# Moving the latents' modulation columns one product later in a diffusion backbone layer on one Trainium2 core

## The reference

```python
m_x = split(silu(c) @ w_ada + b_ada, 9)        # shift, scale, gate of three blocks, latents
m_c = split(silu(c_ctx) @ w_ada + b_ada, 9)    # the same for the context
x   = x   + 0.5 * m_x[2] * swiglu(modulate(rmsnorm(x, g0), m_x[0], m_x[1]), ffn1_w1, ffn1_w2)
ctx = ctx + 0.5 * m_c[2] * swiglu(modulate(rmsnorm(ctx, g0), m_c[0], m_c[1]), ffn1_w1, ffn1_w2)
px  = modulate(rmsnorm(x, g1), m_x[3], m_x[4]) @ w_in      # -> q, k, v, g, u, vg
pc  = modulate(rmsnorm(ctx, g1), m_c[3], m_c[4]) @ w_in
ret_x = retention_readout(bidir_retention(rope(q), rope(k), v, states of ctx), g)
gm_x  = gelu(u) * (w_s @ layernorm(gelu(vg)) + b_s)        # per chunk of 128 positions
x   = x + m_x[5] * (concat(ret_x, gm_x) @ w_out)
x   = x + 0.5 * m_x[8] * swiglu(modulate(rmsnorm(x, g2), m_x[6], m_x[7]), ffn2_w1, ffn2_w2)
return rmsnorm(x, final_g)
```

## Time and profile before

| | |
|---|---|
| timed runs | 2182.26, 2183.96, 2188.76 us |
| profiled execution | 2187.05 us, span 2185.2 us |
| TensorE busy | 2101.5 us (96%) |
| VectorE busy | 1539.6 us (70%) |
| ScalarE busy | 681.3 us (31%) |
| GpSimd busy | 747.6 us (34%) |
| mean granted TensorE clock | 0.980 |

### The profile page before, as it was taken

The page is one execution under the profiler, slowest core; times in us unless marked ns, Lnnn a source line. Parts: engine busy times, 40 slices in busy tenths (PEclk is TensorE's granted clock), DMA queues, the critical chain, the costliest instruction groups (busy, mean ns, idle before and its releaser), DMA issues.

```text
span 2185.2 us, 28724 instructions
## 1 busy us (share of the span) xinstructions
PE 2101.5 (96%) x10408; PEld 1754.0 (80%) x10408; DVE 1539.6 (70%) x2198; ACT 681.3 (31%) x1063; POOL 747.6 (34%) x452
## 2 busy tenths in 40 slices
PE   8999989999999999989999968998999999999997
PEld 4999978888888888878888866776888888888886
DVE  4987687777777777686353465578777777777767
ACT  4234432332233323273202111235323232232322
POOL 1000053443344433263322121365434443344431
PEclk9999999999999999989999988999999999999998
DMA  7964311111101111131010332420110111101112
GB/s 301 359 239 145 126 60 46 58 58 58 53 33 58 58 58 57 68 122 58 5 54 12 134 105 89 148 105 18 58 57 30 58 58 58 58 29 58 58 39 77
DMA packets 35161, 181.35 MB, mean 83 GB/s; under 512 B 4112, under 2 KB 5392, under 8 KB 18832
## 3 DMA queue, kind: packets, MB, share of 16 engines
q1 hardware_dynamic: 32784, 163.57, 20.4%
q10 hardware_dynamic: 2304, 16.78, 2.2%
HBM read 175.09 MB, written 5.24 MB: 83 GB/s over the span
## 4 chain that ended last, share of the span: by engine, by line
PE 86%; DVE 9%; issue 1%; ACT 1%; DMA 1%; POOL 0%; SPq 0%; DVEq 0%; ACTq 0%
PE PS L1843 14%; PE PS L1845 14%; PE PS L1844 14%; PE PS L2005 12%; PE PS L2007 12%; PE PS L2006 12%; PE PS L1948 3%; DVE AS L1313 1%; DVE X L1471 1%; PE PS L1903 1%; DVE V L1779 1%; PE PS L2202 1%; DVE ACC L1180 1%; PE PS L1881 0%; DMA AW<-w_units 0%
## 5 line engine op out<-in xcount | busy, mean ns | idle before, releaser
L1471 DVE SCALAR_TENSOR_TENSOR X<-PS,GATE,X 128x512 f32<-128x512 f32 x704 | 484.5, 746 | 186.7 <-PE PS L1845 186.7
L638 POOL TENSOR_TENSOR WVL<-WR,WVH 128x512 fp32r<-128x512 f32 x168 | 238.2, 1428 | 561.2 <-ACT WVH L849 560.4
L1843 PE MATMUL PS<-PXH,W2H 128*128 128x512 f32 x672 | 266.1, 396 | 10.2 <-DVE X L1471 10.2
L2005 PE MATMUL PS<-HH,WVH 128*128 128x512 f32 x672 | 265.3, 395 | 0.0
L1845 PE MATMUL PS<-PXH,W2L 128*128 128x512 f32 x672 | 264.9, 394 | 0.0
L2007 PE MATMUL PS<-HH,WVL 128*128 128x512 f32 x672 | 264.0, 393 | 0.0
L1844 PE MATMUL PS<-PXL,W2H 128*128 128x512 f32 x672 | 263.4, 392 | 0.0
L2006 PE MATMUL PS<-HL,WVH 128*128 128x512 f32 x672 | 262.7, 391 | 0.0
L638 POOL TENSOR_TENSOR WVL<-ST,WVH 128x512 fp32r<-128x512 f32 x125 | 186.1, 1489 | 83.2 <-ACT WVH L849 83.0
L1843 PE MATMUL PS<-HH,WH 128*128 128x512 f32 x416 | 170.4, 410 | 4.3 <-DVE WL L1621 4.3
L612 POOL TENSOR_TENSOR WL<-WR,WH 128x2048 fp32r<-128x2048 f32 x20 | 93.2, 4661 | 216.2 <-ACT WH L772 216.2
(11 more groups left out here) (258 smaller groups left out, 4410.1 us busy)
## 6 DMA issues: line engine op xcount, KB each, us to landing
WR<-w_units SPq DMA_DIRECT2D x89, 1024.0 KB, 5.4
W2R<-w_units SPq DMA_DIRECT2D x44, 512.0 KB, 3.5
AW<-w_units ACTq DMA_DIRECT2D x16, 1024.0 KB, 5.0
AW<-ada_units SPq DMA_DIRECT2D x11, 1024.0 KB, 13.7
W2RB<-w_units SPq DMA_DIRECT2D x22, 512.0 KB, 3.6
AW<-w_units SPq DMA_DIRECT2D x8, 1024.0 KB, 6.6
X<-x SPq DMA_DIRECT2D x2, 2048.0 KB, 9.9
out<-OUT SPq DMA_DIRECT2D x2, 1024.0 KB, 4.2
```

The lines of the kernel that those rows point to most:

```text
L638: pool.tensor_tensor(WVL[:, slot], src, WVH[:, slot].bitcast(F32), ALU.subtract).then_inc(s_wl, 1)
L1471: dve.scalar_tensor_tensor(xv, y_bank(n)[:, :], GATE[:, 2 * f, d, 0:1], xv, ALU.mult, ALU.add).then_inc(s_fyd, 1)
L1843: pe.matmul(dst, wh, xh, start=first, stop=False)
L2005: pe.matmul(bank[:, :], wh, xh, start=first, stop=False, skip_group_check=True)
```

## The change

Five things change, all in the handling of units 20 to 35:

1. The columns of a unit are made ahead of the entry behind the second whole product after its sums, where the short `mixed` entries are not counted (`columns_at`). Before it was ahead of the second entry.
2. The sums go into two buffers in turn (`AS2[a % 2]`), so the sums of a unit wait for the columns of the unit two before, and no longer for those of the one before.
3. The load of a unit is issued by ScalarE in two halves of 512 KB, one entry after the slot of the unit before (`load_at`; two after it for one entry), each half as soon as the sums have passed the same half of the unit before. The sums wait for each half.
4. The columns go to bank 7 in place of bank 6; to make that possible the scale of norm (2, 1) goes to bank 6 and a wait of TensorE for the last unit's modulation moves from norm_sum(2, 1) to the start of the second feed-forward block.
5. The slots are other ones. Unit 20 has its sums at the third `g` product, unit 26 at the fourth `vg` product of unit 13, there between the statistics and the normalization.

```diff
--- before.py
+++ after.py
@@ -57,8 +57,8 @@
 ADA_SUMS = (15, 14, 14, 14) + (11,) * 7 + (9, 12, 12, 12, 13)
 NRING = 6
-ADA_SLOTS = ((11, 0), (11, 2), (12, 0), (12, 2), (13, 0), (13, 2), (14, 0), (14, 3), (14, 6), (15, 0), (15, 3), (15, 6),
-             (16, 0), (17, 0), (18, 0), (19, 0))
+ADA_SLOTS = ((10, 5), (11, 0), (11, 2), (12, 0), (12, 2), (13, 0), (13, 3), (14, 3), (14, 7), (15, 1), (15, 4), (15, 7),
+             (16, 1), (17, 1), (18, 1), (19, 1))
 NM = 7
 A0, B_, A1, D_ = 0, 1, 7, 6
@@ -108,6 +108,26 @@
 ADA_AT = {ADA_CTX + n: FIRST_FILL[i] + k for n, (i, k) in enumerate(ADA_SLOTS)}
+def columns_at(a):
+
+    n, whole = ADA_AT[a], 0
+    while whole < 2:
+        n += 1
+        whole += FILLS[n][1] != "mixed"
+    return n + 1
+
+
+def load_at(a):
+
+    if a == ADA_CTX:
+        return FILL["yscale", HEADS - 1, 1] + 1
+    return ADA_AT[a - 1] + (2 if FILLS[ADA_AT[a - 1]][1:] == ("vg", 1, 0) else 1)
+
+
+ADA_COLUMNS = {columns_at(a): a for a in ADA_AT}
+ADA_LOADS = {load_at(a): a for a in ADA_AT}
+
+
 SCALED = {p: [(1, 2 * (p - 11) + k) for k in range(2)] for p in range(11, 15)}
@@ -130,7 +150,7 @@
 def sums_count(a):
-    return a - 8 + len(ADA_DVE) + 1
+    return min(a, ADA_CTX - 1) - 8 + len(ADA_DVE) + 1 + 2 * max(0, a - ADA_CTX + 1)
 def layer(nc, x, ctx, c2, ada_units, w_units, w2_units, b_ada, norm_g, final_g, decay, ws, bs, cosine, sine, consts, powers, ident, out):
@@ -221,7 +241,7 @@
         V2 = at("V2", [P, NCH, UC], F32, R + 57344)
         DG2 = at("DG2", [P, 4, P], F32, R + 67584)
         AW2 = at("AW2", [P, KT, UC], F32, R + 69632)
-        AS2 = at("AS2", [P, UC], F32, R + 68608)
+        AS2 = [at(f"AS2_{j}", [P, UC], F32, R + o) for j, o in enumerate((65536, 68608))]
         DM = at("DM", [P, HEADS, P], F32, R + 65536)
         TMP = at("TMP", [P, 2, TB], F32, R + 69632)
         S0 = at("S0", [P, 2, HEADS, P], F32, R + 73728)
@@ -365,7 +385,7 @@
         def scale_bank(place, b):
-            return {(1, 0): PS[0], (1, 2): ST_BANK, (2, 2): PS[4], (3, 2): PS[0]}.get((place, b), RB_BANK)
+            return {(1, 0): PS[0], (1, 2): ST_BANK, (2, 1): ST_BANK, (2, 2): PS[4], (3, 2): PS[0]}.get((place, b), RB_BANK)
         def last_release(bank):
             return release(max(n for n in range(len(FILLS)) if n % NRING == bank))
@@ -1079,18 +1099,19 @@
             def latent_unit(u):
-                if u == ADA_CTX:
-                    act.wait_ge(s_fill, FILL["yscale", HEADS - 1, 1] + 1)
-                else:
-                    act.wait_ge(s_adv, sums_count(u - 1))
-                act.dma_start(AW2[:, :, :], ada_source(u)).then_inc(s_first[u % 8], 16)
+                for half in range(2):
+                    k = slice(4 * half, 4 * half + 4)
+                    if u == ADA_CTX:
+                        act.wait_ge(s_fill, FILL["yscale", HEADS - 1, 1] + 1)
+                    else:
+                        act.wait_ge(s_adv, sums_count(u - 1) - 1 + half)
+                    act.dma_start(AW2[:, k, :], ada_source(u)[:, k, :]).then_inc(s_first[half], 16)
             n_gate = 0
             for n, (i, name, a, b) in enumerate(FILLS):
                 ps, free = PS[n % NRING], s_free[n % NRING]
-                for u in range(ADA_CTX, N_ADA):
-                    if n == (ADA_AT[u - 1] + 2 if u > ADA_CTX else FILL["yscale", HEADS - 1, 1] + 1):
-                        latent_unit(u)
+                if n in ADA_LOADS:
+                    latent_unit(ADA_LOADS[n])
                 if n == FIRST_FILL[i] and 5 <= i < len(MIX_UNITS) - 1:
                     mix_high(i + 1)
                 if name in ("cv", "state0", "v", "vg", "kt", "o", "g", "u"):
@@ -1252,7 +1273,7 @@
             def latent_mods(a):
                 c = 16 + 2 * (a % 4)
                 dve.wait_ge(s_col, a + 1)
-                dve.tensor_tensor(MODS[:, bass.ts(a, 2), 0], PS[6][:, c:c + 2], BA[:, bass.ts(a, 2), 0],
+                dve.tensor_tensor(MODS[:, bass.ts(a, 2), 0], RB_BANK[:, c:c + 2], BA[:, bass.ts(a, 2), 0],
                                   ALU.add).then_inc(s_mods, 1)
             def gain(place):
@@ -1300,18 +1321,23 @@
             def latent_sums(a):
-                links = 15 * sums_count(ADA_CTX - 1) + 7 * (a - ADA_CTX)
-                if a > ADA_CTX:
-                    dve.wait_ge(s_col, a)
-                dve.wait_ge(s_first[a % 8], load_count(a))
+                sums, links = sums_count(a - 1), 15 * sums_count(ADA_CTX - 1) + 6 * (a - ADA_CTX)
+                acc = AS2[a % 2]
+                if a > ADA_CTX + 1:
+                    dve.wait_ge(s_col, a - 1)
                 for k in range(KT):
+                    if k % 4 == 0:
+                        dve.wait_ge(s_first[k // 4], 16 * (a - ADA_CTX + 4))
                     w, c = AW2[:, k, :], CS[:, k, 0:1]
                     if k == 0:
-                        ins = dve.tensor_scalar(AS2[:, :], w, c, None, ALU.mult)
+                        ins = dve.tensor_scalar(acc[:, :], w, c, None, ALU.mult)
                     else:
-                        dve.wait_ge(s_asum, links + k)
-                        ins = dve.scalar_tensor_tensor(AS2[:, :], w, c, AS2[:, :], ALU.mult, ALU.add)
-                    ins.then_inc(s_adv if k == KT - 1 else s_asum, 1)
+                        if k == 4:
+                            dve.wait_ge(s_adv, sums + 1)
+                        else:
+                            dve.wait_ge(s_asum, links + k - k // 4)
+                        ins = dve.scalar_tensor_tensor(acc[:, :], w, c, acc[:, :], ALU.mult, ALU.add)
+                    ins.then_inc(s_adv if k % 4 == 3 else s_asum, 1)
             dve.wait_ge(s_const, 16 * 6)
             def block_low(b):
@@ -1699,6 +1725,12 @@
                 dve.wait_ge(sums, 3)
                 dve.tensor_tensor(s4, a12, s2, ALU.subtract).then_inc(sums, 1)
+            def unit_sums(n):
+
+                for u in ADA_AT:
+                    if ADA_AT[u] == n:
+                        latent_sums(u)
+
             n_rope = n_gate = 0
             for n, (i, name, a, b) in enumerate(FILLS):
                 ps, free = PS[n % NRING], s_free[n % NRING]
@@ -1771,6 +1803,7 @@
                     link(ins)
                     if b == 3:
                         dve.tensor_scalar(MS[:, 16:32], MV[:, :, 1], EPS, None, ALU.add).then_inc(s_lv, 1)
+                        unit_sums(n)
                         dve.wait_ge(s_lr, a + 1)
                         for c in range(NCH):
                             for g in range(2):
@@ -1808,20 +1841,20 @@
                         dve.wait_ge(s_lo[1], unit_count(DVE_UNIT))
                         dve.wait_ge(s_raw1, 16)
                         second_sums()
-                for u in range(ADA_CTX, N_ADA):
-                    if n == ADA_AT[u] + 2:
-                        latent_mods(u)
-                        if u == 23:
-                            gate(1)
-                            dve.wait_ge(s_coef, 7)
-                        if u == 31:
-                            gain(2)
-                            dve.wait_ge(s_coef, 8)
-                        if u == N_ADA - 1:
-                            gate(2)
-                            dve.wait_ge(s_coef, 9)
-                    if n == ADA_AT[u]:
-                        latent_sums(u)
+                if n + 1 in ADA_COLUMNS:
+                    u = ADA_COLUMNS[n + 1]
+                    latent_mods(u)
+                    if u == 23:
+                        gate(1)
+                        dve.wait_ge(s_coef, 7)
+                    if u == 31:
+                        gain(2)
+                        dve.wait_ge(s_coef, 8)
+                    if u == N_ADA - 1:
+                        gate(2)
+                        dve.wait_ge(s_coef, 9)
+                if (name, b) != ("vg", 3):
+                    unit_sums(n)
             add_square(2, 2, KT - 1)
             norm_mean(2, 2)
             norm_diagonal(2, 2)
@@ -1849,8 +1882,6 @@
                 pe.wait_ge(s_acc, 8 * (j + 1))
                 if j:
                     pe.wait_ge(s_ms, j)
-                if (place, b) == (2, 1):
-                    pe.wait_ge(s_mods, N_ADA)
                 for c in range(n // P):
                     ins = pe.matmul(ST_BANK[:, c:c + 1], acc[:, c * P:(c + 1) * P], ONES[:, 0:1], start=True, stop=True)
                 ins.then_inc(s_st, 1)
@@ -1888,7 +1919,7 @@
                 pe.wait_ge(s_mods, a)
                 for t in range(2):
                     c = 16 + 2 * (a % 4) + t
-                    ins = pe.matmul(PS[6][:, c:c + 1], AS2[:, t * P:(t + 1) * P], ONES[:, 0:1], start=True, stop=True)
+                    ins = pe.matmul(RB_BANK[:, c:c + 1], AS2[a % 2][:, t * P:(t + 1) * P], ONES[:, 0:1], start=True, stop=True)
                 ins.then_inc(s_col, 1)
             def first_product(n):
@@ -2067,6 +2098,7 @@
                         ins.then_inc(done, 1)
                 if f:
+                    pe.wait_ge(s_mods, N_ADA)
                     for bank in (A0, B_):
```

(5 more changed lines are left out.)

## The result

The changed kernel took 2154.06 us (median of 4 runs, 2153.48 to 2157.13) beside 2184.03 us before, a ratio of 0.9864 [0.9852, 0.9876]: 30 us faster, where 33 were forecast.

What follows compares the result with a forecast made beforehand. TensorE, busy 2101.5 of 2185.2 us, was held by columns waiting for VectorE's sums and by half clock after; 37.6 + 13.4 - 2 - 4 - 5 - 1 - 5 = 34, said as 33: median 2151 us, 8 in 10 between 2139 and 2163.

Steps and rivals of the forecast that it cites:

- The columns' waits and their half clock: TensorE at the columns, mixer's second half: 37.6 us of waits and 13.4 us of half clock behind them would go.
- Unit 25: Columns of unit 25, at the normalization of unit 12: a new wait of 2 us for VectorE's sums.
- Unit 17: Out products of weight unit 17: a wait for GpSimd's low half, between 2 and 7 us, taken as 4.
- bare sum: Chain durations added without GpSimd and VectorE interfering: 2.0 us late at unit 17, 2.5 to 4.2 at unit 18.
- Unit 18: Low half of weight unit 18: 2.5 to 4.2 us late, up to 5 more beside GpSimd, taken as 5.
- Later units: Weight units after 18: 11 us of room for a chain of some 9; 1 us of waits together.
- Half clock after the new waits: TensorE after three new waits of about 2 us or more: 5 us lost at half clock.
- The prediction's 8: TensorE's busy time would shrink by some 8 us (13.4 - 5), as less is at half clock.
- The loads at 0: Loads in halves: cost 0, bounds -1 and +4; VectorE's 6.7 us of load waits neither vanish nor grow much.
- rival C: Second halves of loads land 3 us late and delay VectorE's other entries: gain 26 us, 2158; chance 0.07.
- Rival B: ScalarE's order bounds the out products, units 17 to 20 each late by 5 us: gain 20, 2164; chance 0.11.
- The ceiling A: New waits stay at their lower bounds, under the size that costs the clock: gain 44 us, 2140; chance 0.13.

Runs made afterwards that it cites:

- Experiment 1: The changed kernel with the columns back ahead of the second entry behind the sums, new slots, halves and two buffers kept: ratio 1.0014.
- experiment 2: The kernel before with only the later columns, two sum buffers and the other bank; old slots, whole loads: ratio 0.9925.
- experiment 5: The changed kernel with one buffer of sums, which wait for the columns of the unit just before: ratio 0.9864.
- experiment 4: The changed kernel with whole loads of 1 MB in the new slots in place of halves: ratio 0.9874.
- experiment 3: The changed kernel with the old slots; halves, two buffers and later columns kept: ratio 0.9873.
- 8: The changed kernel with ScalarE's high half ahead of the load and GpSimd's low half in four instructions: ratio 0.982, 2148.34 us.
- experiment 6: The changed kernel with ScalarE making the high half of the next weight unit before it waits for the load: ratio 0.9853.
- 11: The kernel of experiment 8 with the columns of unit 31 one entry later: ratio 0.9846.
- 12: The kernel of experiment 8 with the columns of units 31 and 32 one entry later: ratio 0.984.

## Why the prediction was right, and where it was off

*The columns' waits and their half clock (37.6 + 13.4).* Right: line 1922 has 2.6 us left. Experiment 1 shows that without the later place none of it goes. But the place is not enough: with the old slots and whole loads (experiment 2) only 17 of the 30 us came. The prediction had a term of 0 for the loads and none for the slots. Each may indeed be undone for 2 to 3 us of stretch, but both together for 12.8. And it named the second buffer as what permits the later place, which experiment 5 contradicts for these slots.

*Unit 25: forecast 2, measured 2.1.* At unit 26, where the 10.1 us stood, nothing is left. The prediction gave this to the sums' new place ahead of the normalization; either cause is enough, since the new slots alone left 0.7 us there (experiment 1) and the later columns alone 1.6 (experiment 2).

*Unit 17: forecast 4, between 2 and 7; measured 5.6 + 0.5.* This term was mis-sized. The bare sum gave 2.0, and nearly all of the rest is one instruction: the mixed entry's product at 1322.03 took 4.64 us in place of 0.69, 3.95 us more. VectorE's chain, from the mixed entry at 1320.03 to the end of the sums of unit 31 at 1350.9, took 30.9 us where the sum had 26.7. To the 3.95 come 1.30 us that it stood ahead of that instruction for ScalarE's read of the u product, and 0.5 for the next; the 1.4 us of slack that the sum had before the next mixed entry are taken off. The result is 5.58 and 0.46 us, 6.04. I had the price (4.6 us at most, 1 for the late read) and the place right and took a middle value for it. The Trainium skill's rule (SBUF — State Buffer, "Who interferes with whom"), a lock held for the whole instruction, would have given 7 by my sum; the durations agree with it: 4.64, 4.58 and 4.68 us beside instructions of 4.60, 4.50 and 4.60.

*Unit 18: forecast 5, measured 4.9.* Chain and TensorE both came later than the bare sum. VectorE's sums ended 11.5 us after the start of unit 17's products and not 8.2, since its four low parts took 3.46 + 2.38 us beside GpSimd's. The low half was there at +18.5 (15.6), TensorE at +13.6 (11.4 to 13.1). So the hit is partly luck: both ends moved by more than the forecast was off. The full price of the lock, 9 by the prediction's sum, was not reached here.

*Later units: forecast 1, measured 1.4,* at unit 20.

*Half clock after the new waits: forecast 5, measured about 5.* I count from the end of each wait to ScalarE's next read (unit 25) or to the next columns (units 17 and 18), and take off what the same work needs at full clock: 8.0 for 6.4 us after unit 25, 13.1 for 10.9 after unit 17, 12.4 for 10.9 after unit 18: 1.6 + 2.2 + 1.5 = 5.3. The window 1357 to 1372 had a granted clock of 0.82:

```profile
1357.00:1372.00 15.00, 13.63 (x52) 11.05 (x52) 11.73 (x16) 3.04 (x4) 7.02 (x6) 0.82 0.41 126
```

*Sum.* 51.0 - 2.1 - 6.0 - 4.9 - 1.4 - 5.3 = 31.3 against 29.9 in the stretch. This sum mixes two views: the 37.6 us in it are seen from the weight loads, the new waits (14.4) from the products. From the loads the new ones are 15.2 us (12.1 and 3.1), which takes 0.8 of the 1.4 us; 0.6 stay open. Seen from the products alone 33.6 - 14.4 = 19.2 us of waits went, just what the idle time fell by. The other 4.0 of the 37.6 us had counted as busy time, 0.8 of the new waits do so again, and with 13.4 - 5.3 us of half clock that makes 11.3 for the fall in busy time, measured 10.7. The prediction's 8 had left the 4.0 out. Of the miss of 3 us, 2 are at unit 17 and 0.4 at unit 20.

*The loads at 0, bounds -1 and +4.* Right in the new slots: halves against whole are 2 us of stretch (experiment 4), and the list of waits after has no row for VectorE and this load. That the 6.7 us of VectorE's waits for loads would neither vanish nor grow much was wrong: they vanished. DMA issues of the page after:

```profile
AW<-w_units ACTq DMA_DIRECT2D x32, 512.0 KB, 4.2
```

The Trainium skill's advice of 1 MB or more (DMA: Bandwidth & Descriptors, "Bandwidth") spoke for rival C. A half took 4.2 us to land, more than the 3.5 of the prediction, and a whole 5.0; yet no kernel was slower with halves, in any of three pairs: experiment 3 beside 2, the changed kernel beside 4, and 8 beside 10.

*What the prediction didn't have.* VectorE is busy for 18.4 us more in this stretch, 15.6 of them at the squares' additions, which now run beside low halves (4.58 and 4.68 us above). This goes with the slots and not with the columns: VectorE was busy for 176.3 us with the new slots and the columns at their old place (experiment 1), and for 162.6 and 165.5 with the old slots (2 and 3). Each of the larger waits that are left is behind a chain through VectorE's queue, and I take that to be why neither another order on ScalarE (experiment 6) nor later columns (11, 12) bring more. Rival B put the blame on ScalarE's order at units 17 to 20; the waits came at 17, 18 and 20, with ScalarE waiting up to 12.0 us for sums, but taking that order away gained 1 us. The ceiling A (gain 44) was not reached by any kernel; the best has 36.3 us of stretch.
